# Mixture-of-experts rounds: 96 tokens in plain float32, tokens stationary in four column positions, in place of 128 tokens in three float32r products

## The reference

```python
def moe_swiglu(h, router, we_gate, we_up, we_down):        # h: 256 x 1024
    top_v, top_i = lax.top_k(h @ router, 2)                 # 8 experts, each token goes to 2
    top_w = jax.nn.softmax(top_v, axis=-1)
    for e in range(8):                                      # FFE = 3584
        out = out + gates[..., e:e+1] * ((silu(h @ we_gate[e]) * (h @ we_up[e])) @ we_down[e])
```

## Time and profile before

| | |
|---|---|
| median of 3 runs | 2038.55 us (2037.59 to 2039.62) |
| profiled execution, span | 2036.7 us |
| time outside the span (median less span) | 1.85 us |
| busy: PE / PEld / DVE / ACT / POOL | 1997.2 / 1643.3 / 1644.6 / 1296.2 / 49.7 us |
| read from HBM | 537.11 MB |
| granted TensorE clock, mean | 0.997 |

### The profile page before, as it was taken

The page is one execution under the profiler, slowest core; times in us unless marked ns, Lnnn a source line. Parts: engine busy times, 40 slices in busy tenths (PEclk is TensorE's granted clock), DMA queues, the critical chain, the costliest instruction groups (busy, mean ns, idle before and its releaser), DMA issues.

```text
span 2036.7 us, 29701 instructions
## 1 busy us (share of the span) xinstructions
PE 1997.2 (98%) x9978; PEld 1643.3 (81%) x9978; DVE 1644.6 (81%) x2285; ACT 1296.2 (64%) x1720; POOL 49.7 (2%) x61
## 2 busy tenths in 40 slices
PE   8999999999999999999999999999999999999998
PEld 7796889668888878888758888888888888888887
DVE  6578787786777976665658989899998989999898
ACT  2321456454445665555548888887888888788886
POOL 0000000000000000002000000000000000000000
PEclk9999999999999999999999999999999999999999
DMA  9778744356553245563248999999999999999996
GB/s 322 163 288 298 298 155 145 104 170 202 187 185 104 83 145 186 186 187 114 85 165 312 397 350 407 353 406 382 360 393 356 392 363 399 387 360 396 347 405 239
DMA packets 275464, 548.71 MB, mean 269 GB/s; under 512 B 29485, under 2 KB 81206, under 8 KB 275126
## 3 DMA queue, kind: packets, MB, share of 16 engines
q1 hardware_dynamic: 266189, 528.46, 70.7%
q0 software_dynamic: 3984, 14.68, 2.5%
q10 hardware_dynamic: 5208, 4.49, 1.2%
HBM read 537.11 MB, written 10.48 MB: 269 GB/s over the span
## 4 chain that ended last, share of the span: by engine, by line
PE 92%; DVE 6%; ACT 1%; issue 1%; DMA 0%; SPq 0%; ACTq 0%; DVEq 0%
PE sum L1728 13%; PE bank L1710 10%; PE bank L1712 10%; PE bank L1711 10%; PE bank L1281 7%; PE sum L1263 6%; PE bank L766 5%; PE bank L1283 3%; PE sum L830 2%; PE bank L931 2%; PE bank L784 1%; PE sum L1353 1%; PE bank L1696 1%; PE sum L810 1%; PE sum L1742 1%
## 5 line engine op out<-in xcount | busy, mean ns | idle before, releaser
L3379 DVE TENSOR_TENSOR x_lo<-ring,x_hi 128x1024 fp32r<-128x1024 f32 x672 | 780.9, 1220 | 45.1 <-ACT x_hi L2380 24.8
L2380 ACT ACTIVATE x_hi<-ring 128x1024 fp32r<-128x1024 f32 x648 | 667.0, 1058 | 118.0 <-PE bank L1712 63.0
L1710 PE MATMUL bank<-x_hi,hg_hi 128*128 128x512 f32 x896 | 354.2, 395 | 1.6 <-DVE xtr L3336 1.6
L1712 PE MATMUL bank<-x_hi,hg_lo 128*128 128x512 f32 x896 | 349.4, 390 | 0.0
L1711 PE MATMUL bank<-x_lo,hg_hi 128*128 128x512 f32 x896 | 348.9, 389 | 0.0
L2598 DVE TENSOR_TENSOR w_lo<-ring,w_hi 128x1024 fp32r<-128x1024 f32 x130 | 155.9, 1223 | 77.8 <-ACT w_hi L2114 76.7
L1281 PE MATMUL bank<-hT_hl,w_hi 128*128 128x512 f32 x608 | 216.5, 399 | 1.9 <-DVE hT_hl L2575 1.3
L2114 ACT ACTIVATE w_hi<-ring 128x1024 fp32r<-128x1024 f32 x130 | 136.7, 1059 | 125.5 <-PE sum L1263 66.2
L1712 PEld LDWEIGHTS bank<-x_hi,hg_lo 128*128 128x128 f32 x896 | 168.2, 188 | 35.9
L1710 PEld LDWEIGHTS bank<-x_hi,hg_hi 128*128 128x128 f32 x896 | 168.3, 188 | 35.0 <-DVE xtr L3336 1.7
L1711 PEld LDWEIGHTS bank<-x_lo,hg_hi 128*128 128x128 f32 x896 | 168.4, 188 | 33.5
(11 more groups left out here) (648 smaller groups left out, 3229.6 us busy)
## 6 DMA issues: line engine op xcount, KB each, us to landing
ring<-in_sw_we_gate SPq DMA_DIRECT2D x114, 1024.0 KB, 7.3
ring<-in_sw_we_up SPq DMA_DIRECT2D x112, 1024.0 KB, 7.5
ring<-in_sw_we_down SPq DMA_DIRECT2D x112, 1024.0 KB, 7.4
ring<-in_w_in SPq DMA_DIRECT2D x36, 1024.0 KB, 7.5
ring<-in_w_ff SPq DMA_DIRECT2D x32, 1024.0 KB, 5.5
ring<-in_ada_w SPq DMA_DIRECT2D x24, 1024.0 KB, 10.2
ring<-in_w_out SPq DMA_DIRECT2D x12, 1024.0 KB, 6.1
ring<-in_cv_w_gate SPq DMA_DIRECT2D x11, 1024.0 KB, 5.1
```

The source lines that it names most:

```text
L1710: mm(ps[b][:, :], hg_hi[:, k, :], hi[:, cols], start=(k == 0), stop=False)
L1712: last = mm(ps[b][:, :], hg_lo[:, k, :], hi[:, cols], start=False, stop=(k == KC - 1))
L2380: go(f(x_hi[:, hp % MSLOTS, :], ring[:, s, lo:lo + PIECE // 2], ACT.Copy), c.sig("hi_ready", hp))
L3379: v.tensor_tensor(x_lo[:, hp % MSLOTS, :], ring[:, s, lo:lo + PIECE // 2], x_hi[:, hp % MSLOTS, :].bitcast(F32), ALU.subtract).then_inc(c. ...
```

## The change

A round is now CAP = 96 tokens. An expert with more than 96 tokens gets a second round, one with more than 192 a third; the tables of rounds grow from 3 to 5 spare places. With the counts above there are again 8 rounds.

All expert products are plain float32 matmuls. The 96 tokens are three tiles x of 32; each tile is stationary with 32 columns. A matmul writes its 32 rows to partitions 32q to 32q+31, and the four positions q take four different stretches of weight columns as moving operand: for gate and up a quarter of a piece's 2048 or 1536 columns (512 or 384 each), for down four different blocks of 256 columns. So PE puts out four matmuls in a row that differ in q. The splits into `x_hi` and `x_lo` on ACT and DVE are gone.

SP loads 48 pieces a round into 16 slots (the ring's 7, `x_even`, and 8 of `x_odd`): gate and up by k-block and half, in rows of 8 KB (1 MB) and 6 KB (0.75 MB), down likewise. Piece j waits until PE has used piece j-16 at all four positions (`x_used0` to `x_used3`). Pieces i and i+1 share a landing semaphore.

ACT takes silu of the gate sums in place of the half (3 tiles of 512, then of 384), DVE multiplies by up, PE turns the product (`turn_gated`), ACT and DVE copy it to `actT`. `ey` is three tiles of 128 x 256, the quarter rows go to `xrows` by three indirect transfers a round. After the loop the last result takes the same way, and SP then copies `xrows` to the output in DRAM.

```diff
-EXTRA = (2 * S) // (P + 1)
+CAP, TILES = 96, 3
+EXTRA = (2 * S) // (CAP + 1)
+XWIDE = (2048, 1536)
+XSLOTS = 16
+ROUND_PIECES = [(w, k) for w in ("gate0", "gate1", "up0", "up1") for k in range(KC)] + [("down0", x) for x in range(8)] + [("down1", x) for x in range(8)]
...
+                    for j, (name, k) in enumerate(ROUND_PIECES):
+                        i, half = j % XSLOTS, int(name[-1])
+                        for q in range(4):
+                            sp.wait_ge(*(c.at(f"x_used{q}", j - XSLOTS) if j >= XSLOTS else c.before(f"x_used{q}", j + len(ROUND_PIECES) - XSLOTS)))
...
+                        sp.dma_start(xslot(i)[:, 0:XWIDE[half]], src).then_inc(c.sem(xlanded(i)[0]), 16)
...
+                sp.wait_ge(c.sem("last_added"), 16 * TILES)
+                sp.dma_start(out.rearrange("a s d -> (a s) d"), xrows[0:S, :]).then_inc(c.sem("out_stored"), 16)
+                sp.wait_ge(c.sem("out_stored"), 16)
...
+                def wide_sums(name, half, between=lambda: None):
+                    n = XWIDE[half] // 4
+                    for k in range(KC):
+                        j = ROUND_PIECES.index((f"{name}{half}", k))
+                        if k == 4:
+                            between()
...
+                        w = came(j)
+                        for x in range(TILES):
+                            for q in range(4):
+                                last = mm(wide_banks[half][x][32 * q:32 * q + 32, 0:n], hg[:, k, 32 * x:32 * x + 32], w[:, n * q:n * (q + 1)],
+                                          start=(k == 0), stop=(k == KC - 1))
+                                if x == TILES - 1:
+                                    last.then_inc(c.sig(f"x_used{q}", j).sem, 1)
...
+                def down_sums(half, between):
+                    n = XWIDE[half] // 512
...
+                    for p in range(4):
...
+                        for i in range(n):
+                            for x in range(TILES):
+                                for q in range(4):
+                                    piece, at_ = divmod((4 * i + q) * 256, XWIDE[half])
+                                    o = (acc[2][32 * q:32 * q + 32, 256 * x:256 * x + 256] if x < 2 else acc[3][32 * q:32 * q + 32, 0:256])
+                                    last = mm(o, actT[half][:, x, i, 32 * p:32 * p + 32], w[piece][:, at_:at_ + 256], ...)
...
+                wide_sums("gate", 0)
+                wide_sums("gate", 1, rows_step)
...
+                wide_sums("up", 0)
...
+                wide_sums("up", 1, lambda: turn_gated(0))
+                pe.wait_ge(*c.at("ey_ready"))
+                down_sums(0, lambda: turn_gated(1))
+                down_sums(1, turn_rows)
...
-                        go(f(x_hi[:, hp % MSLOTS, :], ring[:, s, lo:lo + PIECE // 2], ACT.Copy), c.sig("hi_ready", hp))
...
+                    for x in range(TILES):
+                        do(f(gated[half][:, x, :], wide_banks[half][x][:, 0:n], ACT.Silu), c.sig("gate_taken", half, x))
...
-                        v.tensor_tensor(x_lo[:, hp % MSLOTS, :], ring[:, s, lo:lo + PIECE // 2],
-                                        x_hi[:, hp % MSLOTS, :].bitcast(F32), ALU.subtract).then_inc(c.sig("lo_ready", hp).sem, 1)
...
+                for x in range(TILES):
+                    g.indirect_dma_start(xquads, bass.IndirectOffsetOnAxis(ap=targeti[:, x:x + 1], axis=0), ey[:, x, :], None, compute_op=ALU.add)\
+                        .then_inc(c.sig("rows_added", x, by=16).sem, 16)
```

More of the change, by code:

```diff
@@ L261, in __init__ @@
         self.c, self.known, self.n, self.number, self.freed = count, known, 0, {}, {}
-        self.slot, self.landing, self.halves = [0] * RING, {}, {}
+        self.slot, self.landing, self.halves, self.first = [0] * RING, {}, {}, 0
     def free(self, key, signal):
@@ L436, in program, with xslot, xlanded @@
         xrows = nc.dram_tensor("xrows", (S + P, D), F32, kind="Internal").ap()
+        def xslot(i):
+            return ring[:, (W.first + i) % RING, :] if i < RING else x_even[:, :] if i == RING else x_odd[:, i - 8, :]
+        def xlanded(i):
+            s = (W.first + (i // 2 * 2 if i < 8 else i // 2 * 2 - RING)) % RING
+            return (f"landed{s}", W.slot[s]) if i < 14 else ("pair_landed", 0)
         def U(unit, *dims, off=0):
@@ L650, in _ @@
             if upto >= 5:
[L651 to L658, removed]
-                        else:
-                            w, (_, g, h) = gate if key[0] == "xgate" else up, key
-                            piece(key, (shaped(4, 512), w[e, :, 4 * h:4 * h + 4, g * 512:(g + 1) * 512]))
-                    assert len(ROUND_PIECES) == 6 * RING and HALVES % MSLOTS == 0
+                W.first = W.n
@@ L1699, in widen @@
[L1699 to L1710, removed]
-                            mm(ps[b][:, :], hg_hi[:, k, :], lo[:, cols], start=False, stop=False)
-                            last = mm(ps[b][:, :], hg_lo[:, k, :], hi[:, cols], start=False, stop=(k == KC - 1))
-                        if q < 3:
-                            s = c.sig("half_used", hp)
-                            last.then_inc(s.sem, 1)
-                        else:
-                            s = done(last, key, g)
-                        W.half_free(hp, s)
@@ L2347, in _ @@
                 return
-            for hp in range(AHEAD):
-                if hp % 2 == 0:
-                    act.wait_ge(*W.ready(ROUND_PIECES[hp // 2]))
-                s, lo = W.place(ROUND_PIECES[hp // 2]), (hp % 2) * (PIECE // 2)
-                go(f(x_hi[:, hp, :], ring[:, s, lo:lo + PIECE // 2], ACT.Copy), c.sig("hi_ready", "first", hp))
             do(f(aT[:, 510:511], ones[:, 0:1], ACT.Sqrt))
@@ L2362, in _ @@
                 do(f(rt[:, 2, t, :], rt[:, 0, t, :], ACT.Exp, bias=xtr[:, t, 0:1]), c.sig("exp_done", "router") if t else None)
-            for q in range(2):
-                act.wait_ge(*J.full("hgfirst", q))
-                do(f(flat(hg_hi[:, 4 * q:4 * q + 4, :]), ps[J.bank("hgfirst", q)][:, :], ACT.Copy), c.sig("gather_high", "first", q))
+            copy(hg[:, 0:4, :].rearrange("p a b -> p (a b)"), ("hgfirst", 0), 4 * CAP)
+            do(f(aT[:, 510:511], ones[:, 0:1], ACT.Copy), c.sig("hg_taken", "first"))
@@ L2418, in _ @@
-                high_next(AHEAD)
+                last_piece = len(ROUND_PIECES) - 1
+                for q in range(4):
+                    act.wait_ge(*c.before(f"x_used{q}", last_piece))
+                act.wait_ge(*c.before("rows_added", TILES - 1))
+                act.wait_ge(*c.before("targets_set"))
+                for x in range(TILES):
+                    do(f(ey[:, x, :], down_banks[x], ACT.Copy, scale=gate_of[:, x:x + 1]), c.sig("ey_ready") if x == TILES - 1 else None)
+                for half in range(2):
+                    n = XWIDE[half] // 4
+                    for q in range(4):
+                        act.wait_ge(*c.at(f"x_used{q}", ROUND_PIECES.index((f"gate{half}", KC - 1))))
+                    for x in range(TILES):
+                        do(f(gated[half][:, x, :], wide_banks[half][x][:, 0:n], ACT.Silu), c.sig("gate_taken", half, x))
```

430 lines of the change are left out of this document (165 added, 265 removed).

## The result

The changed kernel takes 2055.16 us (median of 4 runs, 2049.76 to 2059.41), the kernel before 2038.18 in the same session (4 runs): ratio 1.0081, interval 1.0063 to 1.0098, 0.8% slower. The forecast was 32 us faster. The profiled execution has a span of 2054.6 us.

The account below looks back on a forecast made before the run. PE's matmul stream was taken to bound the kernel. Start 1075.1 + 8 rounds x 114.1 + tail 16 gave a span of 2003.9 us, plus 1.85 for the median of runs: 2006 us, range 1987 to 2068.

Parts of the forecast that it names:

- Waits and branch as before: 0.5: Term of PE's round: waits and the loop's branch keep costing 0.5 us a round, as in the kernel before.
- The round itself: PE's work in one new round, summed to 114.1 us, 5.0 less than before.
- DVE's and ACT's splits worth nothing: Removing 84 ACT copies and 84 DVE subtractions a round gains nothing, since they bound nothing.
- DMA not the bound: A round's 44.04 MB of reads plus scatter and gather take 109 us, under PE's 114.
- Start +0.5: Before the first round: DVE's longer chain ends at about 1075.1, where PE starts at 1074.57 today; +0.5 us.
- Tail 16: After the last round: copy, three scatters, landing and DRAM-to-DRAM transfer in line take 16 us, +7.5; ends 11 and 22.
- The rivals: Four positions not keeping pace (0.27), DMA becoming the bound (0.07), more rounds from an expert over 96 tokens (0.02).
- The break-even of the first: Round time, 118.2 us, at which slow positions cancel the gain: 11 ns on each of 360 steps of four.
- The chance of 0.25 for slower: Chance given to a slower kernel, beside 0.69 for faster and 0.06 for the same.
- the first rival: The four positions do not keep pace in the matmul steps: at 74 ns a pair, 2114 us; chance 0.27.

Follow-up runs that it names:

- a_flat: Changed kernel with PE's loop over the rounds written out eight times, no branch back: 2004.6 us, ratio 0.9832 to the kernel before.
- a_by2: Changed kernel with two rounds in one pass of PE's loop, four passes: 2026.09 us, ratio 0.9936 to the kernel before.
- b_by2_tail: Kernel before, two rounds a pass of PE's loop, 16 matmuls of 4 columns added ahead of each branch: 2063.23 us; same added work without branch 2040.86.
- the pads: b_pad1 and b_pad15: kernel before with semaphore increments added ahead of PE's matmuls to lengthen the loop body; 2038.86 and 2153.7 us.
- a_early: a_flat with a first round that starts without waiting for DVE's whole chain, two filler matmuls bridging: 2002.56 us, ratio 0.9819 to the kernel before.
- b_by2: Kernel before with two rounds in one pass of PE's loop, four passes: 2038.63 us, ratio 1.0002.
- b_pad1: Kernel before with one unused semaphore increment ahead of each of a round's 504 matmuls, 1702 instructions a round: 2038.86 us, one run.
- b_pad15: Kernel before with three unused semaphore increments to every two matmuls, 1955 instructions a round: 2153.7 us, one run.

## Why the prediction was wrong

- **The step that failed** is "Waits and branch as before: 0.5". It stood for 4 us in 913, taken over from a loop whose body is held by PE to one of 2.5 times its length. What it measured is 6.8 us a turn: seven pauses, 33.1 us together, and 14.7 us for the half clock behind them (the 200 records behind the seven pauses take 163.5 us, and 7 x 21.25 = 148.8 at full clock). The cause, the fetch at a branch back to a head that is no longer held, is shown by a_flat (both gone), a_by2 (by the number of branches), b_by2_tail (bare once the cover is short) and the pads (by the length alone).
- **The round itself** was right: 113.75 us in a_flat and a_early against 114.1 forecast. The parts hold: down's 336 matmuls are 672 records (a plain float32 matmul has two: L1719 has 5376 in the trace after, for 8 x 336 matmuls, and as many weight loads, where the 224 transposes of L1696 before have 224 and the 896 float32r matmuls of L1712 have 896), and they pass in 10.36 + 18.27 + 7.91 = 36.5 us against 36.3, and 200 records of gate, 50 steps with 512 columns, in 21.25, 0.425 a step. The four positions start side by side, 36.5 / 672 = 54 ns a pair throughout, so a step of four takes 0.217 us where one full-width record takes 0.216.
- **DVE's and ACT's splits worth nothing, DMA not the bound**: right. 396 GB/s over a round of a_flat, with no idle time of PE in it; after the change SP's queue waited for PE, 88 us of a round.
- **Start +0.5** was too small: 1078.91 in the profile after, +4.3 on the 1074.57 of the earlier trace rows. The gather of the first rows (L1635), on which all of this waits, began at 1070.04, where before (L1645) it began at 1067.42: 2.6 of the 4.3 lie ahead of it. That part can be scatter from run to run: this start lies between 1065.6 and 1071.3 in the seven traces of the kernel before and its variants, and between 1067.3 and 1071.9 in the five of the changed one. The rest is DVE's chain: 8.6 us from the gather's start to its last operation (1070.04 to 1078.66), where 1075.1 - 1067.4 = 7.7 had been counted; its 29 operations took 0.25 us each, not 0.22. The first gate then began at half clock (0.50 from 1078.91 to 1081), which the sum had left out: 24.08 us in place of 21.25.
- **Tail 16**: 14.9 (2039.7 to 2054.6). The sum of the profile: 1078.9 + 960.8 + 14.9 = 2054.6, where the prediction had 1075.1 + 912.8 + 16. The 960.8 are 8 x 113.75 + 33.1 + 14.7 + 2.8, to 0.2 us.
- **The rivals.** None of the named ones came. The break-even of the first, 118.2 us a round, was passed (960.8 / 8 = 120.1), but not by its mechanism: it looked for the extra time in every step of the stream, and it sat in one spot between the streams. The chance of 0.25 for slower was there for another reason than the one that came, and that 2055 lies within the stated range of 1987 to 2068 is luck: its upper part was made for the first rival. That a_flat takes 2004.6 and the forecast was 2006 owes something to errors that cancel (start, rounds and tail).

## What to carry to other kernels

Count the instructions of a loop's body before you make its matmuls smaller (this case shows it for PE; no other engine's body was tried). Here 1702 were held by PE and 1955 were not, and the larger body of the changed kernel cost a pause of 4 to 6 us a turn plus about 2 us of half clock; with some 4 us of issued matmuls ahead of the branch (b_by2) next to nothing was left of it. Writing the loop out removed it: straight code was fetched ahead at no cost. And look at the turn of a loop as a place of its own: a sum over the stream of matmuls says nothing about it.

## What the runs showed of the hardware

- A branch back takes 0.21 us where the head of the loop is held, 3.8 to 4.6 us where it is not in variants of the kernel before, and 4.9 to 6.7 in the changed one. Read in the trace: the first packet of instructions starts 2.1 us behind the branch in b_by2_tail (1311.06, 1313.14) and 3.3 in the changed kernel (1314.84, 1318.14); both packets take 0.9 to 1.0 us, and from the packet's end to that of the branch it is 1.4 us in both. The same holds at 22 of the 23 branches of this kind in the traces: 1.4 to 4.3 us until the packet starts, then 2.3 to 2.4 us until the branch ends (at the first turn of the changed kernel, where two packets start together, 4.2). So what varies is how long the packet waits to start; whether it waits behind the longer rows of the weights was not tried.
- At the branch PE's sequencer is 17 matmuls ahead in the kernel before and 20 records in the changed one (16 once): 3.7 us with 512-column float32r matmuls, 1.0 us with narrow ones. It is 7 with one increment ahead of each matmul (b_pad1), 0 or 1 with three to two (b_pad15), and 6 to 8 behind the short matmuls.
- The 32 records of the 16 short matmuls pass in 0.44 us, 14 ns a pair with the last one's end in it, and their starts lie 8 ns apart on average: narrow pairs of 4 columns go much faster than the 54 ns a pair of the down steps with 256 columns, so it is not the issue of pairs that sets those 54.
